# Two transformer blocks on one core: an MLP with weights stationary, another launch order, one rotation for both halves, a conv projection fed by pairs

## The reference

```python
def token_mixer(h, cos, sin, ...):
    z = h @ w_in
    u_glu, q_lat, kv_lat, k_r, gate_logits = jnp.split(z, IN_SPLIT, axis=-1)
    u = ua * jax.nn.sigmoid(ub)                       # ua, ub: halves of u_glu
    u = causal_depthwise_conv(u, conv_w, conv_b)      # 31 taps, 1024 channels
    y_a = jax.nn.silu(layer_norm(u, ...)) @ w_conv_out
    q = rms_norm_2(q_lat, q_norm_g) @ w_uq            # 8 heads, 128 plain + 64 rotated
    q_rope, k_rope = apply_rope(q_rope, cos, sin), apply_rope(k_r, cos, sin)
    y_b = mla_attention(q_nope, q_rope, k_nope, k_rope, v) @ w_attn_out
    return (g_a * y_a + g_b * y_b) @ w_out
...
y = jnp.square(jax.nn.relu(h @ w_mlp_in)) @ w_mlp_out   # 1024 -> 4096 -> 1024
x = x + gate2 * rms_norm_2(y, g_post_mlp)
```

## Time and profile before

| | |
|---|---|
| median of 3 runs | 1151.19 us (1149.23 to 1151.77) |
| profiled execution | 1153.75 us, span 1151.6 us |
| TensorE busy | 1108.2 us |
| VectorE, ScalarE busy | 818.9, 574.1 us |
| mean granted clock of TensorE | 0.995 |

### The profile page before, as it was taken

How to read it: one execution, slowest core, us unless ns; L and a number is a source line. 1 busy time by engine, 2 the same in 40 slices (tenths; PEclk the granted TensorE clock), 3 DMA queues, 4 the chain that set the end, 5 groups by cost and what they waited for, 6 DMA issues and landing times.

```text
span 1151.6 us, 20521 instructions
## 1 busy us (share of the span) xinstructions
PE 1108.2 (96%) x8408; PEld 939.3 (82%) x8408; DVE 818.9 (71%) x1154; ACT 574.1 (50%) x730; POOL 42.0 (4%) x48
## 2 busy tenths in 40 slices
PE   8899999999999896899999999999989999999997
PEld 7788888889777686777788888798968788999996
DVE  4655444548498556869999988999989867545554
ACT  4646633445555444464343357465556756444443
POOL 0000000000000410101111100000000000000000
PEclk9999999999999999999999999999999999999999
DMA  9595556544334211468999974464530553554632
GB/s 318 165 259 193 171 182 219 180 157 139 110 110 139 52 22 41 141 227 301 342 336 352 353 231 124 121 222 150 179 119 10 190 173 135 169 200 154 210 112 108
DMA packets 129219, 204.88 MB, mean 178 GB/s; under 512 B 11176, under 2 KB 86717, under 8 KB 129150
## 3 DMA queue, kind: packets, MB, share of 16 engines
q1 hardware_dynamic: 121716, 176.58, 46.9%
q0 software_dynamic: 6560, 25.19, 6.4%
q10 hardware_dynamic: 874, 2.12, 0.5%
HBM read 201.78 MB, written 1.05 MB: 176 GB/s over the span
## 4 chain that ended last, share of the span: by engine, by line
PE 79%; DVE 11%; DMA 4%; ACT 4%; issue 2%; SPq 0%; DVEq 0%; POOL 0%; ACTq 0%
PE ps L692 22%; PE ps L694 21%; PE ps L693 21%; DVE wl L2474 3%; PE ps L1116 2%; DMA raw<-in_ab_w_in 2%; DMA raw<-in_ffn_w_up 2%; PE ps L902 2%; PE ps L769 1%; DVE wide L3143 1%; PE ps L1029 1%; ACT wh L1704 1%; PE ps L1590 1%; PE ps L1148 1%; PE ps L1421 1%
## 5 line engine op out<-in xcount | busy, mean ns | idle before, releaser
L2474 DVE TENSOR_TENSOR wl<-raw,wh 128x2048 fp32r<-128x2048 f32 (+2 forms) x155 | 347.6, 2248 | 129.9 <-ACT wh L1704 129.5
L692 PE MATMUL ps<-wh,xh 128*128 128x512 f32 (+3 forms) x1080 | 400.6, 371 | 9.7 <-DVE wl L2474 5.0
L694 PE MATMUL ps<-wl,xh 128*128 128x512 f32 (+3 forms) x1080 | 392.2, 363 | 0.0
L693 PE MATMUL ps<-wh,xl 128*128 128x512 f32 (+3 forms) x1080 | 391.7, 363 | 0.0
L1704 ACT ACTIVATE wh<-raw 128x2048 fp32r<-128x2048 f32 (+2 forms) x155 | 289.1, 1880 | 100.9 <-PE ps L694 74.9
L692 PEld LDWEIGHTS ps<-wh,xh 128*128 128x128 f32 x1080 | 204.2, 189 | 45.4 <-issue 6.8
L694 PEld LDWEIGHTS ps<-wl,xh 128*128 128x128 f32 x1080 | 203.9, 189 | 31.9
L693 PEld LDWEIGHTS ps<-wh,xl 128*128 128x128 f32 x1080 | 204.2, 189 | 30.8 <-issue 1.0
L692 PE MATMUL ps<-wh,gh 128*128 128x512 f32 x288 | 113.3, 393 | 1.9 <-issue 1.0
L693 PE MATMUL ps<-wh,gl 128*128 128x512 f32 x288 | 112.5, 391 | 0.0
L694 PE MATMUL ps<-wl,gh 128*128 128x512 f32 x288 | 112.4, 390 | 0.0
(11 more groups left out here) (409 smaller groups left out, 1212.1 us busy)
## 6 DMA issues: line engine op xcount, KB each, us to landing
wide<-in_w_ada POOLq DMA_DIRECT2D x24, 1024.0 KB, 9.9
raw<-in_ffn_w_gate SPq DMA_DIRECT2D x44, 512.0 KB, 4.3
raw<-in_ffn_w_up SPq DMA_DIRECT2D x44, 512.0 KB, 5.5
raw<-in_ffn_w_down SPq DMA_DIRECT2D x22, 1024.0 KB, 5.0
raw<-in_w_mlp_in SPq DMA_DIRECT2D x16, 1024.0 KB, 7.3
raw<-in_w_mlp_out SPq DMA_DIRECT2D x16, 1024.0 KB, 5.3
raw<-in_w_in SPq DMA_DIRECT2D x16, 512.0 KB, 4.9
raw<-in_w_in SPq DMA_DIRECT2D x8, 1024.0 KB, 5.1
```

What stands on the lines that cost most here:

```text
L692: pe.matmul(o, lh, rh, start=start, stop=False)
L693: pe.matmul(o, ll, rh, start=False, stop=False)
L694: return pe.matmul(o, lh, rl, start=False, stop=stop)
L2474: v.tensor_tensor(wl[:, s, 0:width], raw[:, s, 0:width], f32(wh[:, s, 0:width]), ALU.subtract).then_inc(lo_ready[s], 1)
```

## The change

- **MLP.** From the third hidden block on, the input product takes a tile of the weights as the stationary operand and moves all 256 positions of xh and xl (`up_turned`). Its result has the hidden channels on the partitions, so the transposes go, and gh and gl are made from hmid. The first two blocks stay as they were. The split of the output weights (slot 2) moves behind the copy to gh on ScalarE, and behind gl on VectorE.
- **Launch.** The first block is loaded by two transfers of 512 KB, the first 1024 columns of its split are done in two steps, and TensorE's first product follows them. The fourth block is issued ahead of pool_w, sgu_gain and the pool masks, the fifth and sixth ahead of c and positions. 14 warm-up products in place of 12.
- **Rotation.** One pass over both halves of the positions, with three-level patterns. Conv taps are placed anew.
- **Conv projection.** SiLU, hi and lo copies by two channel tiles in place of four; TensorE starts the projection's first chunk after each pair.

```diff
+            if name == ("ab_in", IN_ORDER[0], 0):
+                v = flat.rearrange("p (a n) -> p a n", a=4)
+                return [(kblock(SRC[what], name[1] * 512, 512, 0)[:, o, :], v[:, o, :]) for o in (slice(0, 2), slice(2, 4))]
...
             sp.dma_start(W(6, 256, D)[0:CK, :], A["conv_w_2"][0]).then_inc(S("conv_rows"), 16)
+            load_block(plan.order[3])
             sp.dma_start(W3(4, 4, 1024, 512), A["pool_w"][0].rearrange("g c d -> c g d")).then_inc(S("mixw"), 16)
...
-            load_block(plan.order[3])
+            load_block(plan.order[4])
+            load_block(plan.order[5])
             sp.dma_start(ccol, ...)
...
+                def up_turned(s, use, halves=range(2)):
...
+                    for j in halves:
+                        for kt in range(KT):
+                            w = slice(kt * FC + j * P, kt * FC + (j + 1) * P)
+                            m = mm3(ps[:, 4 + s, j * SEQ:(j + 1) * SEQ], wh[:, s, w], wl[:, s, w], xh[:, kt, :], xl[:, kt, :],
+                                    kt == 0, kt == KT - 1)
...
+                def body(c, s_next, use_next):
+                    pe.wait_ge(S("mlp.act"), B("mlp.act") + c)
+                    pe.wait_ge(S("mlp.act"), B("mlp.act") + 1)
+                    up_turned(s_next, use_next)
+                    down(c)
...
+                    act.activation((xh if last else gh)[:, 0:2, :], hmid[:, :, :], ACT.Copy).then_inc(S("mlp.gh"), 1)
+                    if not last:
+                        split_hi(2, uses[2] + c, loads[2] + 16 * c + 16, spared=plan.spared[2])
...
+                    v.tensor_tensor(lo[:, 0:2, :], hmid[:, :, :], f32(hi[:, 0:2, :]), ALU.subtract).then_inc(S("mlp.gl"), 1)
+                    if not last:
                         split_lo(2, uses[2] + c)
...
-            for _ in range(12):
+            for _ in range(14):
...
-            for name, n in [(("uq", 1), 7), (("uq", 2), 7), (("uq", 3), 9), (("ukv", 0), 9), (("ukv", 1), 0)]:
+            for name, n in [(("uq", 1), 7), (("uq", 2), 7), (("uq", 3), 5), (("ukv", 0), 2), (("ukv", 1), 0)]:
...
+            src = qraw.rearrange("p t (h x c) -> p t h x c", x=2, c=32)
+            dst = ro[:, :, 0:576].rearrange("p t (h x c) -> p t h x c", x=2, c=32)
...
+            v.tensor_tensor(dst[:, :, :, 0, :], src[:, :, :, 0, :], cs, ALU.mult)
...
             split(("attn_out", 0, 0))
-            conv(7)
+            conv(16)
...
-                conv(5)
+                conv(5 if i else 2)
...
+            for j in range(4):
+                v.wait_ge(S("cv.xh"), B("cv.xh") + j + 1)
+                o = slice(2 * j, 2 * j + 2)
+                v.tensor_tensor(xl[:, o, :], cv[:, o, :], f32(xh[:, o, :]), ALU.subtract).then_inc(S("cv.xl"), 2)
+                if j == 1:
                     attention_gated(1)
                     split(("conv_out", 0, 1))
```

More of the change, by code:

```diff
@@ L935, in _ @@
             pe.wait_ge(S("mix0.xl"), B("mix0.xl") + 2)
-            pe.wait_ge(S("in0.lo"), B("in0.lo") + 1)
             s0, o0 = plan.at["ab_in", 1, 0][0], [ps[:, t, :] for t in range(NT)]
-            half(s0, range(0, 2), o0, 512, True, False)
+            for kt in range(2):
+                pe.wait_ge(S("in0.lo"), B("in0.lo") + kt + 1)
+                half(s0, range(kt, kt + 1), o0, 512, kt == 0, False, kt)
             pe.wait_ge(S("mix0.xl"), B("mix0.xl") + 4)
@@ L1660, in mixed_transposes @@
                     m.then_inc(S("ym.T"), 1)
-            linear("conv_out", "cv.xl", 2, free=lambda c: pe.wait_ge(S("yb"), B("yb") + 2 * (c + 1)),
+            pe.wait_ge(S("yb"), B("yb") + 2)
+            o = [ps[:, t, :] for t in range(NT)]
+            for k in range(2):
+                s = arrive(("conv_out", 0, k))
+                for j in range(2):
+                    pe.wait_ge(S("cv.xl"), B("cv.xl") + 4 * k + 2 * j + 2)
+                    m = half(s, range(4 * k + 2 * j, 4 * k + 2 * j + 2), o, 512, k + j == 0, k + j == 2, 2 * j)
+                m.then_inc(w_used[s], 1)
+            linear("conv_out", "cv.xl", 2, c0=1, free=lambda c: pe.wait_ge(S("yb"), B("yb") + 2 * (c + 1)),
                    after={(1, 0): lambda: mixed_transposes((0, 1))})
@@ L1824, in up, with rows_body @@
                     split_hi(s, uses[s] + use, loads[s] + 16 * use + 16, spared=plan.spared[s])
-                def body(c, s, use, more):
-                    if isinstance(c, int) and c == 0:
+                def rows_body(c):
+                    if c == 0:
                         split_hi(2, uses[2], loads[2] + 16, spared=plan.spared[2])
-                    act.wait_ge(w_used[s], free[s] + use + 1)
[L1830 to L1836, removed]
-                        up(s, use + 1)
[L1838 to L1843, removed]
@@ new lines, in rows_body @@
+                    act.wait_ge(w_used[c], free[c] + 1)
+                    if c:
+                        act.wait_ge(S("mlp.h"), B("mlp.h") + c)
+                    act.activation(silu[:, :, :], ps[:, 4 + c, :].rearrange("p (t n) -> p t n", t=NT), ACT.Relu)\
+                       .then_inc(S("mlp.act"), 1)
+                    if c:
+                        up(1, 1)
+                        split_hi(2, uses[2] + 1, loads[2] + 32, spared=plan.spared[2])
+                    act.wait_ge(S("mlp.mT"), B("mlp.mT") + c + 1)
@@ new lines, in rows_body, with body @@
+                    act.wait_ge(w_used[2], free[2] + c)
+                    act.activation(gh[:, 0:2, :], ps[:, 6, :].rearrange("p (a n) -> p a n", a=2), ACT.Copy).then_inc(S("mlp.gh"), 1)
+                    if c == 0:
+                        up(0, 1)
+                def body(c, s, use):
+                    last = isinstance(c, int) and c == NMLP - 1
+                    act.wait_ge(w_used[s], free[s] + use + 1)
+                    act.wait_ge(w_used[s], free[s] + 1)
+                    act.wait_ge(S("mlp.h"), B("mlp.h") + c)
+                    act.wait_ge(S("mlp.h"), B("mlp.h") + 1)
+                    act.activation(silu[:, :, :], ps[:, 4 + s, :].rearrange("p (a n) -> p a n", a=2), ACT.Relu).then_inc(S("mlp.act"), 1)
+                    if last:
+                        split_hi(0, uses[0] + NMLP // 2, loads[0] + 16 * (NMLP // 2) + 16)
+                    elif not isinstance(c, int):
+                        up(s, use + 1)
+                    act.wait_ge(S("mlp.h"), B("mlp.h") + c + 1)
+                    act.wait_ge(S("mlp.h"), B("mlp.h") + 1)
@@ L2631, in mlp_loop, with rows_body @@
                 uses, _ = plan.at["mlp"]
-                def body(c, s, use, more):
-                    if isinstance(c, int) and c == 0:
+                free = [n - m for n, m in zip(uses, plan.spared)]
+                def rows_body(c):
+                    if c == 0:
                         split_lo(2, uses[2])
@@ new lines, in rows_body, with body @@
+                    v.tensor_tensor(gl[:, 0:2, :], ps[:, 6, :].rearrange("p (a n) -> p a n", a=2), f32(gh[:, 0:2, :]), ALU.subtract)\
+                     .then_inc(S("mlp.gl"), 1)
+                    if c == 0:
+                        split_lo(0, uses[0] + 1)
+                def body(c, s, use):
+                    last = isinstance(c, int) and c == NMLP - 1
+                    v.wait_ge(S("mlp.act"), B("mlp.act") + c + 1)
+                    v.wait_ge(S("mlp.act"), B("mlp.act") + 1)
+                    v.wait_ge(S("mlp.gl"), B("mlp.gl") + c)
+                    v.wait_ge(S("mlp.gl"), B("mlp.gl") + 1)
+                    v.tensor_tensor(hmid[:, :, :], silu[:, :, :], silu[:, :, :], ALU.mult).then_inc(S("mlp.h"), 1)
+                    if last:
+                        split_lo(0, uses[0] + NMLP // 2)
+                    elif not isinstance(c, int):
+                        split_lo(s, uses[s] + use + 1)
+                    v.wait_ge(S("mlp.gh"), B("mlp.gh") + c + 1)
+                    v.wait_ge(S("mlp.gh"), B("mlp.gh") + 1)
+                    hi, lo = (xh, xl) if last else (gh, gl)
+                    v.tensor_tensor(lo[:, 0:2, :], hmid[:, :, :], f32(hi[:, 0:2, :]), ALU.subtract).then_inc(S("mlp.gl"), 1)
+                    if not last:
+                        split_lo(2, uses[2] + c)
```

157 lines of the change are left out of this document (67 added, 90 removed).

## The result

The changed kernel takes 1141.27 us (median of 5 runs, 1137.10 to 1144.59) against 1151.19 before (5 runs, 1149.23 to 1152.47): ratio 0.9912, 95% interval 0.9892 to 0.9932. The profiled execution has that median too: 1141.27 (span 1139.2) where the one of before had 1153.75, 12.5 us less; the forecast's sum was 12.4. From median to median it is 9.9 us where 12.4 were forecast; the forecast was 1138.8, and its range of 1133.5 to 1143.5 holds the 1141.27.

A forecast was written before the change was run, and what follows sets the result against it. TensorE, busy 96% of the span, was taken as the bound. Launch 0.4, rotation and conv projection 5.9 and MLP 6.1 sum to 12.4 us: 1153.75 to 1141.35 profiled, less 2.56 gives median 1138.8; range 1133.5 to 1143.5.

The forecast's parts named there:

- Rival (c): MLP loop: it becomes bound by late output weights, making the whole 6.8 us slower, 1158 us; chance 0.04.
- The circle's margin: MLP loop: the output weights' lo part is ready about 10.4 us, needed at 11.2, leaving 0.8 us.
- rival (d): MLP: weights stationary changes the pace; at 0.146 us a matmul (672 of them) the whole gain is gone; chance 0.01.
- the queue behind a late load: Launch: one DMA engine lags and serves transfers in order, so the fifth block still lands at 32.3 us.
- the work ahead of the scaling: Launch: the fifth block's split stands ahead of v_normed on both engines, so the spatial product starts at 39.5 us.
- the earlier start: Launch: the spatial product starts 1.65 us earlier.
- The price of the slow stretch: Launch: half speed after TensorE's idle time now falls on work that counts, costing about 1.25 us; net gain 0.4.
- The merged operations: Rotation: six operations of 576 elements replace twelve of 288, 0.68 us each; 4.8 us with copies instead of 5.4.
- the taps left over: End of VectorE's list: 5 conv taps, 2.0 us, cost about 0.7 us at the variance product ahead of the norm.
- pairs: Conv projection: SiLU and copies by two tiles start it 0.7 us behind the attention projection, giving 0.7 us back.
- Keeps its clock: Rotation: TensorE waits for nothing at the transposes and stays at full clock; scores start some 5 us earlier.

The follow-up runs named there:

- the two experiments: Changed kernel with the 31 conv-weight rows loaded as two transfers: ratio 0.9891; changed kernel with the gate's scaling ahead of the fifth block's split: 0.9881.
- The kernel with the MLP alone: Kernel before with only the new MLP: 1145.39 us, ratio 0.9944.
- Attention alone: Kernel before with only the merged rotation, moved taps and conv projection by pairs: 1147.97 us, ratio 0.9964.
- the filled kernel: Changed kernel with 24 unused constant products on TensorE ahead of the launch's spatial product: 1141.80 us, ratio 0.9938.

## Why the prediction was right, and where it was not

**MLP.** Right in mechanism and size: 6.1 forecast, 5.94 to 5.98 measured in eight traces, period 11.22, no turns and no idle time of TensorE. Rival (c) stays out, since the output weights land after 5.2 us. The circle's margin was 0.48 us instead of 0.8. In rival (d) a sum is off: over 672 matmuls a pace of 0.139 us, not 0.146, would use up a gain of 12.4; the pace measured is 0.12, which excludes both.

**Launch.** The path was right: fourth block 25.78 (forecast 26.2), fifth 31.64 (32.3), spatial product 38.75 (39.5), and the queue behind a late load and the work ahead of the scaling are shown by the two experiments. Left out was the mask, which ends last (38.70). The term that was mis-sized is the earlier start: 2.4 us at the product and 2.1 to 2.2 at 300 us where 1.65 was forecast. The price of the slow stretch was sized well, 1.25 to 1.5 us for 3.4 us of it against 1.25; but it was taken as certain, and it came in four of six executions, not in the profiled one. With a stretch of 3.4 us in both kernels (free in the old one) the launch is worth 0.7 to 0.95 us to 300 us, without one in the new 2.1 to 2.2; in the runs nothing that 12 of them could show. Forecast 0.4.

**Rotation and conv projection.** The steps came out to 0.3 us: less the 0.96 us by which the stage starts earlier, rotation finished at 837.3 (forecast 837.3), turns at 838.6 (838.8), scores at 842.4 (842.7), first scores read at 845.7 (845.9). The merged operations follow one another in 0.72 us (0.68 forecast). At the end of attention TensorE is 6.05 us ahead (5.9). The two terms behind it were mis-sized, in opposite directions: the taps left over cost 1.2 us at the channel norm (forecast 0.7), pairs won 1.0 back (0.7). The sum agrees, 5.85 against 5.9.

But 1.65 us of the 5.85 hang on the clock. The kernel with the MLP alone has the old rotation and gains exactly that much from 830 to 908, since its profiled execution lacks the slow stretch that the one of before has at 842. "Keeps its clock" was counted as a sure gain of the kernel. Three of four profiled executions with the old rotation have that stretch, two of ten with the new one have one at 850: that may be the edit's doing, but so few executions don't show it. With an undisturbed clock in both kernels the stage gives 4.2 us, with a stretch in both 4.84, and 5.85 only where the old one has it and the new one doesn't. Attention alone has 4.1 us in the runs (2.4 to 5.9), which excludes none of these.

**The sum.** Two sums must be kept apart. In the profiled executions 5.85 + 5.97 + 2.2 less 1.2 that the recurrence gave back (its slow stretch lasted 10.2 us instead of 3.4, its pauses were 1.2 us shorter) is 12.8 at TensorE's last instruction, 12.5 in the time: as forecast, partly by luck. In medians 9.9 us (7.8 to 12.4) was measured; an estimate from like-for-like parts is 5.96 + 4.2 + 0.8 = 11.0. Taking the whole 12.4 off the median was the error of method: the clock of one execution was in it. What is left, about 1 us, lies within the interval.

## To carry to other kernels

A duration from one profiled execution contains that execution's clock: mark the slow stretches in both traces before a difference becomes a gain, and compare parts at markers between them. Where TensorE idles some 3 us the place can be worth more than its idle time (removing the 2.94 us at the launch was worth 2.9 to 3.2 against an execution without a slow stretch there, 4.2 to 4.7 against those with 3.4 us of it). When a transfer is late, look both for the engine that it queues on and for the work that merely stands behind its consumer. A small load like the 31 rows here, issued ahead of big ones, is a cheap thing to try: cutting it in two was worth 3.2 us of the trace.

## What the runs showed that was not expected

- The slow stretches ahead of the tail last 3.4, 6.8 or 10.2 us, at the same places but not in the same executions, and begin during or shortly after idleness: at the launch (eight of ten with 2.8 to 3.0 us idle, none of four without), at about 396 us in the recurrence (ten of 14, after a pause of 1.6 to 2.3 us that the profile puts down to issue; pauses of 1.6, 1.9 and 2.0 us passed without), near 446 us (two of 14, after pauses of 1.4 and 1.6 us), at the old rotation (three of four, 2.3 us idle) and at 850 in the new one (two of ten, 1.3 to 1.7 us idle). A stretch of 3.4 us cost 1.0 us at 850, 1.25 to 1.5 at the launch and 1.65 at the old rotation.
- The pauses put down to issue in the recurrence (384 to 600 us) add up to 7.8 to 12.5 us in 14 profiled executions of kernels that are the same there. From 376 to 700 us the 13 others took between 4.3 us less and 3.6 us more than the one of before. Pauses and slow stretches go with most of that, not with all: for the filled kernel they would give 1.8 us less (slow time counted half), and it took 1.0 more. So a difference of a few us between two single profiles says nothing until this is taken out.
- The kernel with 3 us of idleness filled, even 2.3 us too full, has the steadiest runs: six within 2.7 us (1140.5 to 1143.2), where the 11 with the idle time on the same chip lie within 8.4.
